# Branch C's norm reciprocals all in the first two blocks of branch A, one product piece behind the masked products, and two evacuations in halves

## Chip, core and metric

The kernel runs on one core of one Trainium2 chip. The metric is device time in microseconds (us) of one execution.

## What is computed

One layer of a decoder trunk with four token mixers in parallel, and a final norm; 1024 tokens, model width 1024, branch width 256, all in float32:

```
hn = rmsnorm(x) * (1 + scale) + shift              # scale, shift, gate from c @ w_mod
u  = hn @ w_in                                     # 59 column tiles of 128
ya = rwkv7(...)     * silu(ag)     # branch A: 4 heads of 64, a recurrence over time
yb = hgrn2(...)     * silu(bg)     # branch B
yc = retention(...) * silu(cg)     # branch C: 4 heads, chunks of 128
yd = rglru(...)     * silu(dg)     # branch D
# inside retention, at its end, with 4 heads of 64 columns:
o  = o * rsqrt(mean(o * o over the head) + 1e-6) * ret_norm_g
merged = sum_b sigmoid(mg_b) * (y_b @ w_branch[b]) # 32 merge tiles: 4 branches x 8 column tiles
out = rmsnorm(x + gate * (merged @ w_out)) * final_g
```

## The kernel before

The program is written by hand, one instruction stream per engine, ordered by semaphores. An engine works strictly in the order of its text; a wait holds everything behind it.

**TensorE (PE).** The tiles of `u` are made one after the other in the order of the list `BULK`, two 512-column halves each, with every float32 product taken as three (hn_hi by w_hi, hn_lo by w_hi, hn_hi by w_lo, L590). `project_part(0..3)` makes a quarter of a tile. From `fill` on, a *merge tile* is cut into ten pieces: pieces 0 to 7 are six products each of the gate tile, 8 and 9 are six products each of y @ w_branch (L639). `fill(n)` issues the next n pieces; it is the work that PE does while other engines work on a branch. Piece 0 waits for the evacuation of the tile before it (`s_evac`) and for the weights (`s_w_lo_ready`).

**Branch A** runs in four block pairs, s = 0..3, each over 256 tokens: `rwkv_products` transposes slots (L860, in `turn`), ScalarE (ACT) copies the results to SBUF (L1377, L1380), PE makes the masked products (L884), VectorE (DVE) masks and combines them (L1917 to L1933). `rwkv_inverse` then has five levels: PE products (L910), DVE L1940 or L1943, PE products (L915), DVE L1950 and L1952. After that come four rounds, `rwkv_chunk`, k = 0..3: PE L970 and L978, DVE's two additions L1975 (`s_a_sa_ready`), PE L988 to L997, DVE L1982, L1986, L1989. In round 1 DVE also runs `prep_queries(s + 1)` (L1879 to L1889), in round 2 `prep_keys(s + 1)` (L1897), which sets `s_a_ends_ready`; PE waits for that ahead of the next pair's transposes. A block pair takes 40 pieces, four merge tiles; pair 0 begins in tile 0 at piece 4, so tile 4 starts in round 3 of pair 0.

**Branch C** ends just before pair 0: its eight steps (i = 0..7) go through PE L830 to L848 with a `project_part(i % 4)` in each, ACT copies each result (L1331), and after steps 3 and 7 ACT evacuates the whole tile (`evac(1)`, two instructions at L1235, of which the second tile is Silu). Then ACT squares (L1340), computes the exponentials that branch A needs (`decays(0)`, L1361 to L1366) and takes the roots (L1348). The reciprocals of the roots are eight pieces on DVE, `ret_norm(z)` (L1904), z = 0..3 in slot 16 and 4..7 in slot 17. They are spread over the work of DVE in pair 0.

**GpSimd (POOL)** splits each weight tile into w_hi (a cast, L505) and w_lo (L507), two halves per tile; the first half waits until PE has used up the first half of the tile before (`s_w_first_used`), the second until that tile is done (`s_proj_done`). Behind the weights it splits the branch weights (L515, L517), and at merge tile 0 branch D's y (L476, two instructions). After merge tiles 2 and 3 it finishes branch C in its own order: wait for `s_ret_norm_ready` at 4 and at 8, then L533, L535, L539, L541, L476, a *series* of five operations over 128x1024.

**SyncE** issues the loads of the weights, each behind the split that frees its buffer. ACT and DVE also take the merge tiles' sigmoid (L1257) and products (L1858, or L1861 and L1863).

Of the kernel before, what the change touches and what calls it, by code (L numbers as in the profile page):

```python
# [99 lines left out]
def build(nc, ins, out_d):  # L100
    x_d, w_mod_d, w_in_d, w_branch_d, w_out_d = (ins[n] for n in ("x", "w_mod", "w_in", "w_branch", "w_out"))
    with ExitStack() as ctx:
# [443 lines left out]
        def _(pe):  # L546
# [63 lines left out]
            def fill(count):  # L610

                for _ in range(count):
                    merge_piece(state["piece"] % 10)
                    state["piece"] += 1
# [245 lines left out]
            def rwkv_products(s):  # L862
                if s:
                    pe.wait_ge(s_a_y_ready, 4 * s)
                    pe.wait_ge(s_a_g_ready, 4 * s)
                pe.wait_ge(s_a_ends_ready, s + 1)
                for b in range(2):
                    ts = slice((2 * s + b) * P, (2 * s + b + 1) * P)
                    for q, src in enumerate((12, 13, 4, 5)):
                        last = turn(bank[4 + 2 * b][:, q * P:(q + 1) * P], slot(src)[:, ts])  # L870
                    last.then_inc(s_a_tm1_done, 1)
                    for q, src in enumerate((14, 15, 10, 11)):
                        last = turn(bank[5 + 2 * b][:, q * P:(q + 1) * P], slot(src)[:, ts])
                    last.then_inc(s_a_tm2_done, 1)
                fill(3)
                pe.wait_ge(s_a_tm_ready, 4 * s + 4)
                for b in range(2):
                    for a, src in enumerate((14, 10)):
                        for j in range(2):
                            for c in range(2):  # L880
                                t64 = slice((2 * s + b) * P + c * C, (2 * s + b) * P + (c + 1) * C)
                                for par in range(2):
                                    r = slice(64 * par, 64 * par + 64)
                                    last = mm(bank[4 + 2 * b + par][64 * c:64 * c + 64,  # L884
                                                                    (2 * a + j) * P:(2 * a + j + 1) * P],
                                              slot(src + j)[r, t64], slots[r, j:j + 5:4, t64], start=True, stop=True)
                    last.then_inc(s_a_m_done, 1)
                fill(4)

            def each(f):  # L890
                for b in range(2):
# [255 lines left out]
        def _(act):  # L1147
# [74 lines left out]

            def evac(count):
                for _ in range(count):
                    bi = state["bi"]
                    ct = BULK[bi]
                    banks = (0, 1) if bi % 2 == 0 else (2, 3)
                    for n in range(2):
                        act.wait_ge(s_proj_done, 2 * bi + n + 1)
                        src = bank[banks[n]][:, :]  # L1230
                        if ct in (BF, BF + 1):
                            nc.scalar.activation(b_f_raw[ct - BF][:, halves(n)], src, ACT.Copy).then_inc(s_evac, 1)
                            act.wait_ge(s_evac, after(s_evac))
                        else:
                            nc.scalar.activation(slot(PROJ[ct])[:, halves(n)], src,  # L1235
                                                 ACT.Silu if ct in GATED else ACT.Copy).then_inc(s_evac, 1)
                            after(s_evac)
                    state["bi"] += 1

            def evac_turned(ct, turned):  # L1240
                bi = BULK_AT[ct]
# [85 lines left out]
                after(s_kz_tm_ready)  # L1327
            evac_turned(CV + 1, 1)
            for i in range(NT):
                act.wait_ge(s_ret_o_done, i + 1)  # L1330
                nc.scalar.activation(pair(18)[:, :, i * P:(i + 1) * P],  # L1331
                                     bank[7][:, 0:256].rearrange("p (j t) -> p j t", j=2), ACT.Copy)\
                    .then_inc(s_ret_o_ready, 1)
                act.wait_ge(s_ret_o_ready, after(s_ret_o_ready))
                if i % 4 == 3:
                    evac(1)

            def squares(src, tmp):
                for j in range(2):
# [34 lines left out]
            for s in range(NT // 2):  # L1374
# [29 lines left out]
                for k in range(4):  # L1404
                    n = 4 * s + k
# [147 lines left out]
        def _(dve):  # L1553
# [346 lines left out]
            def ret_norm(z):  # L1900

                dve.wait_ge(s_roots, 4 + z // 2 + 1)
                q = slot(16 + z // 4)[:, 256 * (z % 4):256 * (z % 4 + 1)]
                nc.vector.reciprocal(q, q).then_inc(s_ret_norm_ready, 1)  # L1904
                dve.wait_ge(s_ret_norm_ready, after(s_ret_norm_ready))
# [7 lines left out]
            for s in range(NT // 2):  # L1913
# [22 lines left out]
                for l in range(1, 6):  # L1936
                    dve.wait_ge(s_a_v_done, 5 * s + l)
                    v_new = bank[5][:, 0:256].rearrange("p (n t) -> p n t", t=32)
                    if l < 5:
                        nc.vector.tensor_tensor(v_lev, v_new, table(tb("lev")[:, 32 * l - 32:32 * l], 8), MUL)\  # L1940
                            .then_inc(s_a_v_ready, 1)
                    else:
                        nc.vector.tensor_copy(v_lev, v_new).then_inc(s_a_v_ready, 1)  # L1943
                    dve.wait_ge(s_a_v_ready, after(s_a_v_ready))
                    if l in (1, 4):
                        merge_half(1)
                    dve.wait_ge(s_a_dx_done, 5 * s + l)
                    du = bank[6][:, 0:256].rearrange("p (n t) -> p n t", t=32)
                    if l < 5:
                        nc.vector.tensor_tensor(Ud, Ud, du, ADD).then_inc(s_vector_step, 1)  # L1950
                        dve.wait_ge(s_vector_step, after(s_vector_step))
                        nc.vector.transpose(Td, Ud).then_inc(s_a_x_ready, 1)  # L1952
                        dve.wait_ge(s_a_x_ready, after(s_a_x_ready))
                        if l == 3:
                            merge_half(0)
                    else:
                        dve.wait_ge(s_a_uu_ready, 2 * s + 2)
                        for c in range(2):
                            r = slice(64 * c, 64 * c + 32)
                            done = s_vector_step if c == 0 else s_a_x_ready  # L1960
                            nc.vector.tensor_copy(UU[r, :, 32:64], du[r]).then_inc(done, 1)
                            dve.wait_ge(done, after(done))
                    if s == 0:
                        ret_norm(l - 1)
                for k in range(4):
                    b, c = k // 2, k % 2
                    i, n = 2 * s + b, 4 * s + k
                    rc = slice(64 * c, 64 * c + 64)
                    if s == 0 and k < 3:
                        ret_norm(5 + k)  # L1970
                    dve.wait_ge(s_a_wg_done, n + 1)
                    dve.wait_ge(s_a_u_ready, s + 1)
                    for par in range(2):
                        u = pair(14)[rc, :, i * P + C * par:i * P + C * (par + 1)]
                        nc.vector.tensor_tensor(u, u, bank[6 + par][rc, 0:128].rearrange("p (j v) -> p j v", j=2),  # L1975
                                                ADD).then_inc(s_a_sa_ready, 1)
                    if k == 3:
                        merge()
                    dve.wait_ge(s_a_y_done, 2 * n + 2)
                    dve.wait_ge(s_a_y_part, n + 1)  # L1980
                    y = pair(4)[:, :, n * C:(n + 1) * C]
                    nc.vector.tensor_tensor(y, y, bank[6][:, 256:384].rearrange("p (j t) -> p j t", j=2), ADD)\  # L1982
                        .then_inc(s_a_y_ready, 1)
                    dve.wait_ge(s_a_y_ready, after(s_a_y_ready))
                    dve.wait_ge(s_a_gnew_done, n + 1)
                    nc.vector.tensor_tensor(G, G, bank[5][:, 0:P], ADD).then_inc(s_vector_step, 1)  # L1986
                    dve.wait_ge(s_vector_step, after(s_vector_step))
                    g2 = G.rearrange("p (j v) -> p j v", j=2)
                    nc.vector.tensor_tensor(g2, g2, e_end[:, s % 2, k, :].unsqueeze(2).to_broadcast([P, 2, C]), MUL)\  # L1989
                        .then_inc(s_a_g_ready, 1)  # L1990
                    dve.wait_ge(s_a_g_ready, after(s_a_g_ready))
                    if k == 0:
                        merge()
                    elif k == 1 and s + 1 < NT // 2:
                        prep_queries(s + 1)
                    elif k == 2 and s + 1 < NT // 2:
                        prep_keys(s + 1)
# [268 lines left out]
```

## Time and profile before

| | us |
|---|---|
| median of 3 runs | 1095.77 (1094.17 to 1098.38) |
| the profiled execution | 1097.14 |
| its span, first to last instruction | 1095.0 |
| PE busy | 1058.5 |
| DVE, ACT, POOL busy | 592.4, 304.9, 373.6 |

The span is what the views of the trace show; 2.1 us of the profiled execution lie outside it. Times within views count from the start of the span. PE is TensorE's matmuls, DVE VectorE, ACT ScalarE, POOL GpSimd. A bracket at the end of a row of a timeline is the time for which the engine stood idle before that row, and what released it. L-numbers are lines of the kernel before.

### The profile page before, as it was taken

How to read it: one execution, taken by the hardware profiler on the slowest of the kernel's cores; microseconds unless marked ns; L12 is line 12 of the kernel's file. 1: busy time of each engine (PE TensorE's matmuls, PEld its weight loads, DVE VectorE, ACT ScalarE, POOL GpSimd, SP SyncE). 2: the span in 40 equal slices, each digit the busy share in tenths (PEclk: the TensorE clock that was granted, in tenths of full speed). 3: DMA queues.
4: the chain of work that ended last, by engine and by line, in shares of the span. 5: the costliest groups of instructions: out<-in, count | busy, mean ns of one | idle time of the engine just before them, and what ended most of it. 6: DMA issues, size and time to landing. Idle time of an engine off the chain costs nothing.

```text
span 1095.0 us, 22343 instructions
## 1 busy us (share of the span) xinstructions
PE 1058.5 (97%) x9736; PEld 830.6 (76%) x9736; DVE 592.4 (54%) x976; ACT 304.9 (28%) x497; POOL 373.6 (34%) x343
## 2 busy tenths in 40 slices
PE   7999999999999799999999999999999999999997
PEld 5686787767677677877877777877778777888885
DVE  3768933976455152353442118557777586423543
ACT  5545113321502102202201034244545341001221
POOL 1431543321435421222222232344334239762000
PEclk9999999999999899999999999999999999999999
DMA  9700111210110110110111121120101026412221
GB/s 355 263 21 10 48 49 49 77 29 25 40 28 25 34 41 26 35 41 25 35 41 31 30 68 39 39 59 26 51 26 50 26 86 246 129 36 96 96 77 58
DMA packets 80129, 70.25 MB, mean 64 GB/s; under 512 B 4128, under 2 KB 68896, under 8 KB 80032
## 3 DMA queue, kind: packets, MB, share of 16 engines
q1 hardware_dynamic: 74560, 49.35, 14.6%
q10 hardware_dynamic: 5472, 19.47, 4.8%
q8 instruction: 77, 1.26, 0.5%
q14 instruction: 20, 0.16, 0.0%
HBM read 64.61 MB, written 4.19 MB: 63 GB/s over the span
## 4 chain that ended last, share of the span: by engine, by line
PE 84%; DVE 9%; POOL 3%; DMA 1%; ACT 1%; issue 1%; SPq 1%; ACTq 0%; DVEq 0%; POOLq 0%
PE bank L590 52%; PE bank L1123 8%; PE bank L639 6%; PE bank L691 2%; PE bank L1078 1%; DVE slots L1706 1%; DMA slots<-in_w_mod 1%; PE bank L910 1%; PE bank L915 1%; DVE tab L1924 1%; PE bank L796 1%; DVE stage L1917 1%; PE bank L860 1%; POOL y_lo L476 1%; DVE slots L1690 1%
## 5 line engine op out<-in xcount | busy, mean ns | idle before, releaser
L590 PE MATMUL bank<-hn_hi,w_hi 128*128 128x512 f32 x880 | 360.9, 410 | 10.4 <-POOL w_lo L507 7.6
L590 PE MATMUL bank<-hn_hi,w_lo 128*128 128x512 f32 x880 | 344.6, 392 | 0.0
L590 PE MATMUL bank<-hn_lo,w_hi 128*128 128x512 f32 x880 | 344.6, 392 | 0.0
L505 POOL CAST w_hi<-w_raw 128x512 fp32r<-128x512 f32 x110 | 86.1, 783 | 537.1 <-PE bank L590 537.1
L590 PEld LDWEIGHTS bank<-hn_hi,w_hi 128*128 128x128 f32 x880 | 165.8, 188 | 51.8 <-issue 12.5
L590 PEld LDWEIGHTS bank<-hn_hi,w_lo 128*128 128x128 f32 x880 | 165.9, 189 | 36.4
L590 PEld LDWEIGHTS bank<-hn_lo,w_hi 128*128 128x128 f32 x880 | 166.2, 189 | 33.2 <-issue 1.9
L507 POOL TENSOR_TENSOR w_lo<-w_raw,w_hi 128x512 fp32r<-128x512 f32 x110 | 155.4, 1413 | 8.8
L1257 ACT ACTIVATE stage<-bank 128x512 f32<-128x512 f32 x64 | 38.2, 600 | 208.0 <-PE bank L590 189.4
L1861 DVE TENSOR_TENSOR stage<-stage,bank 128x512 f32<-128x512 f32 x48 | 33.0, 687 | 50.2 <-PE bank L639 48.9
L1235 ACT ACTIVATE slots<-bank 128x512 f32<-128x512 f32 x42 | 24.6, 599 | 123.0 <-PE bank L590 122.9
L639 PE MATMUL bank<-y_hi,w_branch_hi 128*128 128x512 f32 x128 | 51.3, 401 | 0.0
L1123 PE MATMUL bank<-out_w_hi,hn_hi 128*128 128x512 f32 x128 | 49.9, 390 | 0.2 <-DVE hn_lo L2156 0.2
L639 PE MATMUL bank<-y_lo,w_branch_hi 128*128 128x512 f32 x128 | 50.0, 391 | 0.0
L639 PE MATMUL bank<-y_hi,w_branch_lo 128*128 128x512 f32 x128 | 50.0, 390 | 0.0
L1123 PE MATMUL bank<-out_w_lo,hn_hi 128*128 128x512 f32 x128 | 49.8, 389 | 0.0
L1123 PE MATMUL bank<-out_w_hi,hn_lo 128*128 128x512 f32 x128 | 49.8, 389 | 0.0
L1863 DVE TENSOR_TENSOR slots<-slots,stage 128x512 f32<-128x512 f32 x48 | 42.1, 878 | 1.7
L1917 DVE TENSOR_TENSOR stage<-bank,tab 128x512 f32<-128x512 f32 x16 | 9.9, 684 | 41.3 <-PE bank L884 41.3
L2172 DVE TENSOR_TENSOR fin_tmp<-bank,slots 128x512 f32<-128x512 f32 x16 | 11.1, 692 | 38.2 <-PE bank L1123 38.1
L517 POOL TENSOR_TENSOR w_branch_lo<-w_branch,w_branch_hi 128x256 fp32r<-128x256 f32 x32 | 28.0, 875 | 2.6
L691 PE MATMUL bank<-hn_hi,w_hi 128*128 128x512 f32 x64 | 26.4, 413 | 2.4 <-DVE hn_lo L1616 2.4
(320 smaller groups left out, 1546.5 us busy)
## 6 DMA issues: line engine op xcount, KB each, us to landing
w_raw<-in_w_in SPq DMA_DIRECT2D x110, 256.0 KB, 2.8
slots<-in_w_mod SPq DMA_DIRECT2D x16, 512.0 KB, 11.4
slots<-in_x SPq DMA_DIRECT2D x8, 512.0 KB, 9.5
w_branch<-in_w_branch SPq DMA_DIRECT2D x32, 128.0 KB, 2.8
slots<-in_w_mod ACTq DMA_DIRECT2D x8, 512.0 KB, 5.2
slots<-in_w_out ACTq DMA_DIRECT2D x8, 512.0 KB, 6.3
xr<-in_x ACTq DMA_DIRECT2D x8, 512.0 KB, 3.5
out<-xr ACTq DMA_DIRECT2D x8, 512.0 KB, 2.6
```

The source lines that it names most:

```text
L505: nc.gpsimd.tensor_copy(w_hi[p][:, :, :], w_raw[p][:, :, :]).then_inc(s_pool_step, 1)
L507: nc.gpsimd.tensor_tensor(w_lo[p][:, :, :], w_raw[p][:, :, :], w_hi[p][:, :, :].bitcast(F32), ALU.subtract).then_inc(s_w_lo_ready, 1)
L517: nc.gpsimd.tensor_tensor(w_branch_lo[h][:, :, :], w_branch[h][:, :, :], w_branch_hi[h][:, :, :].bitcast(F32), ALU.subtract)\
L590: last = mm(o, w[p][:, k4, :], h[:, k, n * HALF:(n + 1) * HALF], start=(p == 0 and k4 == 0 and q == 0), stop=(p == 1 and k4 == 3 and q == 2))
L639: last = mm(o, w[:, k, :], h[:, k, :], start=(k == 0 and q == 0), stop=(k == 1 and q == 2))
L691: last = mm(bank[q][:, :], w[p][:, k4, cols], h[:, k, n * HALF:(n + 1) * HALF], start=(k == 0 and z == 0), stop=(k == KT - 1 and z == 2))
L1123: last = mm(bank[(2 * tt + n) % 8][:, :], m[tt % 2][:, k * P:(k + 1) * P], w[k][:, n * HALF:(n + 1) * HALF], start=(k == 2 and q == 0), st ...
L1235: nc.scalar.activation(slot(PROJ[ct])[:, halves(n)], src, ACT.Silu if ct in GATED else ACT.Copy).then_inc(s_evac, 1)
L1257: nc.scalar.activation(sig[n], bank[(6 if mi == AHEAD else 0) + n][:, :], ACT.Sigmoid).then_inc(s_evac, 1)
L1861: nc.vector.tensor_tensor(sig[n], sig[n], bank[(4 if mi == AHEAD else 2) + n][:, :], MUL).then_inc(s_vector_step, 1)
L1863: nc.vector.tensor_tensor(o, o, sig[n], ADD).then_inc(s_merged, 1)
L1917: nc.vector.tensor_tensor(kinds(b)[:, par].rearrange("p a j t -> p (a j) t"), bank[4 + 2 * b + par][:, :].rearrange("p (h t) -> p h t", h= ...
```

## The change

The eight reciprocals of branch C are put elsewhere in DVE's order of pair 0: numbers 1 and 3 stand inside levels 2 and 3 of the inverse, between the two products of a level; 0, 2, 4, 5 and 6 follow levels 1 to 5; 7 stands ahead of round 0. Before, 0 to 4 followed the levels, and 5, 6 and 7 stood ahead of rounds 0, 1 and 2. In `rwkv_products`, in all four block pairs, PE issues two pieces ahead of the masked products and five behind, instead of three and four. ACT evacuates the two tiles that are projected during the retention steps in halves: the first half after the copy of step 2 (and 6), the second half ahead of the wait for step 3's (and 7's) result; before, both halves came after the copy of step 3 (and 7).

```diff
@@ rwkv_products (PE)
                     last.then_inc(s_a_tm2_done, 1)
-                fill(3)
+                fill(2)
                 pe.wait_ge(s_a_tm_ready, 4 * s + 4)
...
                     last.then_inc(s_a_m_done, 1)
-                fill(4)
+                fill(5)
@@ ACT
             def evac(count):
                 for _ in range(count):
-                    bi = state["bi"]
+                    evac_halves((0, 1))
+
+            def evac_halves(ns):
+                for bi in (state["bi"],):
                     ct = BULK[bi]
                     banks = (0, 1) if bi % 2 == 0 else (2, 3)
-                    for n in range(2):
+                    for n in ns:
                         act.wait_ge(s_proj_done, 2 * bi + n + 1)
...
-                    state["bi"] += 1
+                    state["bi"] += ns[-1]
...
             for i in range(NT):
+                if i % 4 == 3:
+                    evac_halves((1,))
                 act.wait_ge(s_ret_o_done, i + 1)
...
-                if i % 4 == 3:
-                    evac(1)
+                if i % 4 == 2:
+                    evac_halves((0,))
@@ DVE, branch A, levels l = 1..5
                     if l in (1, 4):
                         merge_half(1)
+                    elif s == 0 and l < 4:
+                        ret_norm(2 * l - 3)
                     dve.wait_ge(s_a_dx_done, 5 * s + l)
...
                     if s == 0:
-                        ret_norm(l - 1)
+                        ret_norm((0, 2, 4, 5, 6)[l - 1])
                 for k in range(4):
...
-                    if s == 0 and k < 3:
-                        ret_norm(5 + k)
+                    if s == 0 and k == 0:
+                        ret_norm(7)
                     dve.wait_ge(s_a_wg_done, n + 1)
```

## Rows read from the trace of the kernel before

**Rows 1.** The page, part 1: busy time, share and instructions, TensorE first.
```profile
PE 1058.5 (97%) x9736; PEld 830.6 (76%) x9736; DVE 592.4 (54%) x976; ACT 304.9 (28%) x497; POOL 373.6 (34%) x343
```
**Rows 2.** PE's waits: for whom, us in total, times, longest us.
```profile
PE bank L590 <- POOL w_lo L507: 7.6, 2, 5.9
...
PE bank L910 <- DVE wa L1933: 2.6, 4, 0.6
```
**Rows 3.** Windows: length, PE, PEld, DVE, ACT, POOL busy, granted clock, DMA share, GB/s.
```profile
260.00:280.00 20.00, 18.34 (x100) 13.58 (x96) 8.83 (x13) 5.69 (x9) 7.30 (x7) 1.00 0.12 33
...
360.00:380.00 20.00, 14.94 (x82) 12.13 (x83) 0.89 (x4) 2.07 (x4) 9.55 (x10) 0.74 0.14 39
```
**Rows 4.** PE's timeline, pair 0, round 3: start, us, operation, idle before.
```profile
357.54 0.50 PE L639 MATMUL bank<-y_hi,w_branch_hi 128*128 128x512 f32 x1
...
365.06 0.76 PE L590 MATMUL bank<-hn_hi,w_hi 128*128 128x512 f32 x1 [5.86 <-POOL w_lo L507]
...
375.99 1.91 PE L860 MATMUL bank<-tab,slots 128*128 128x128 f32 x16
```
**Rows 5.** PE's timeline, pair 1, round 3.
```profile
447.54 0.50 PE L639 MATMUL bank<-y_hi,w_branch_hi 128*128 128x512 f32 x1
...
455.85 1.91 PE L860 MATMUL bank<-tab,slots 128*128 128x128 f32 x16
```
**Rows 6.** POOL's timeline, the second series and the split of merge tile 4.
```profile
351.70 2.37 POOL L533 TENSOR_TENSOR slots<-slots 128x1024 f32<-128x1024 f32 x1 [11.38 <-DVE slots L1904]
...
357.10 2.39 POOL L539 TENSOR_TENSOR slots<-slots 128x1024 f32<-128x1024 f32 x1
...
360.68 2.34 POOL L476 TENSOR_TENSOR y_lo<-slots,y_hi 128x1024 fp32r<-128x1024 f32 x1
...
363.65 1.26 POOL L507 TENSOR_TENSOR w_lo<-w_raw,w_hi 128x512 fp32r<-128x512 f32 x1
```
**Rows 7.** DVE's timeline, pair 0: level 2's addition, two reciprocals, the eighth.
```profile
309.32 0.42 DVE L1950 TENSOR_TENSOR tab<-tab,bank 128x256 f32<-128x256 f32 x1 [1.85 <-PE bank L915]
...
327.91 3.54 DVE L1904 RECIPROCAL slots<-slots 128x256 f32<-128x256 f32 x2
...
349.88 1.75 DVE L1904 RECIPROCAL slots<-slots 128x256 f32<-128x256 f32 x1
```
**Rows 8.** POOL's timeline, pair 1, rounds 0 and 1.
```profile
428.79 0.74 POOL L517 TENSOR_TENSOR w_branch_lo<-w_branch,w_branch_hi 128x256 fp32r<-128x256 f32 x1
...
438.99 1.60 POOL L507 TENSOR_TENSOR w_lo<-w_raw,w_hi 128x512 fp32r<-128x512 f32 x1
```
**Rows 9.** DVE's timeline, pair 0, round 1.
```profile
346.82 0.29 DVE L1989 TENSOR_TENSOR stage<-stage,tab 128x128 f32<-128x128 f32 x1
...
349.08 0.88 DVE L1889 SCALAR_TENSOR_TENSOR slots<-slots,par 128x256 f32<-128x256 f32 x2
```
**Rows 10.** DVE's timeline, pair 1, round 1.
```profile
439.49 1.78 DVE L1889 SCALAR_TENSOR_TENSOR slots<-slots,par 128x256 f32<-128x256 f32 x2
```
**Rows 11.** DVE's timeline ahead of pair 0.
```profile
281.62 1.29 DVE L1879 TENSOR_TENSOR slots<-slots 128x504 f32<-128x504 f32 x1 [4.71 <-ACT slots L1366]
...
285.07 0.69 DVE L1897 TENSOR_TENSOR slots<-slots,tab 128x512 f32<-128x512 f32 x1
```
**Rows 12.** POOL's timeline at the same time: branch D's y.
```profile
277.68 4.70 POOL L476 TENSOR_TENSOR y_lo<-slots,y_hi 128x1024 fp32r<-128x1024 f32 x2
```
**Rows 13.** PE's timeline, pair 0, round 2.
```profile
352.84 0.34 PE L988 MATMUL bank<-stage,slots 64*64 64x64 f32 x4
```
**Rows 14.** The chain that ended last: start, us, what; three pieces of pair 1.
```profile
377.90 4.13 PE bank L590 x18
```
**Rows 15.** PE's timeline, pair 1, level 1.
```profile
390.28 0.75 PE L910 MATMUL bank<-wa,stage 32*32 32x32 f32 x64 [0.64 <-DVE wa L1933]
```
**Rows 16.** PE's timeline, the first fill, and the transposes of pair 0.
```profile
276.97 0.50 PE L590 MATMUL bank<-hn_hi,w_hi 128*128 128x512 f32 x1 [1.66 <-ACT slots L1235]
...
286.03 1.91 PE L860 MATMUL bank<-tab,slots 128*128 128x128 f32 x16
```

## What I expect of the change, and why

> **What bounds the kernel now.** Part 1 of the page comes first: TensorE (PE) is busy for 1058.5 of the 1095.0 us of the span [rows 1], so a change pays only where PE stands still or runs slowly. The table of PE's waits names the places. The longest single one is 5.9 us, for the split of a weight tile on POOL (w_lo, L507); four waits of 0.6 us, 2.6 in all, are for DVE's transpose at L1933 [rows 2]. The table of windows shows the granted clock next: 0.74 between 360 and 380 us, against 1.00 elsewhere, as between 260 and 280 [rows 3]. So the long wait costs twice, once as idle time and once as work at 1.2 GHz instead of 2.4.
>
> I price it by comparing two block pairs of branch A, not from the wait alone. The last round of pair 0 runs from its first merge product at 357.54 to the transposes of the next pair at 375.99, 18.45 us [rows 4]. The same instructions in pair 1, which has no reciprocals of branch C, run from 447.54 to 455.85, 8.31 us [rows 5]. The difference is **10.14 us**; 5.86 of it is the idle time in [rows 4], the other 4.28 the low clock.
>
> Why is the weight split late? POOL's timeline shows it idle for 11.38 us until 351.70, released by DVE's L1904, and then busy with a series of five operations that is over at 360.68 + 2.34 = 363.0. Only then comes the split of merge tile 4, ready at 363.65 + 1.26 = 364.9 [rows 6]. PE starts at 365.06. The eighth reciprocal, `ret_norm(7)`, ends at 349.88 + 1.75 = 351.63 [rows 7]: it is what POOL waits for.
>
> **Part 1: the reciprocals.** Their number (eight) and size stay. In the new order 0 and 2 follow levels 1 and 2, 1 and 3 stand inside levels 2 and 3, 4 and 5 follow levels 3 and 4, 6 follows level 5, and 7 stands ahead of the first round. DVE has 1.85 us of idle before the level's last addition [rows 7]; a reciprocal of 1.75 goes into it, so numbers 1 and 3 cost nothing. If they overran by a tenth, PE still has two pieces of fill before it wants the result. Behind level 5 there are two reciprocals now, 327.91 to 331.45 [rows 7]; they become numbers 6 and 7. So the eighth ends at 331.5 on the clock of before, 20 us earlier, and the ones ahead of rounds 1 and 2 vanish from DVE.
>
> POOL's queue decides how much of this is usable. The first series (after tile 2) needs reciprocals 0 to 3 and can start some 6 us sooner, into time in which POOL was idle. The second stands behind the split of tile 3, whose second half waits for PE to use up tile 2. Pair 1 gives that time undisturbed: the split of the branch weights ends at 428.79 + 0.74 = 429.53 [rows 8], and the last rounds of the pairs are 90.00 us apart [rows 4, 5], so 339.5 here. The series takes 363.0 - 351.7 = 11.3 us [rows 6] and is over at 350.9; the first half of tile 4 is ready near 353. PE wants it after the six products that start at 357.54, so at about 359. **The 5.9 us stall goes, with 6 us to spare, and with it the low clock: -10.1 us.** What is late next is below.
>
> **The collision this makes.** In its new place the second series runs beside `prep_queries(1)` in round 1. Today POOL is idle there. What does DVE pay? The pair L1889, with two operands in SBUF, takes 0.88 us at 349.08, when POOL is idle, but 1.78 at 439.49, when POOL's w_lo runs from 438.99; and that w_lo takes 1.60 instead of the 1.26 at 363.65 [rows 6, 8 to 10]. L1879, issued at 281.62, ends at 282.91, just behind POOL's y_lo, which ends at 282.38 [rows 11, 12]. So they take turns, a whole instruction at a time: DVE ends at the end of POOL's plus its own length less 0.17, and POOL starts about 0.14 before DVE's end.
>
> Worked through: the series starts at 339.6. By the offsets of [rows 6], L539 runs until 347.4 and L541 until 348.5. DVE reaches L1989 at 346.82 [rows 9], is held by L539 and free at 347.5; L1879 ends at 349.0; POOL's y_lo (2.34) at 351.2; L1882 at 351.75; the cast of w_hi (the 0.6 between 363.02 and 363.65) at 352.2; L1884 at 352.7; w_lo (1.26) at 353.9; the pair L1889 at 354.6; the two additions L1975 at 355.1 (0.5, an estimate: each touches half the partitions of an operation like L1989, 0.29). PE wants these additions at 352.84, where it starts L988 [rows 13]. **New wait: +2.3 us.** Bounds: 0, if DVE wins the early turns, because the undisturbed list ends before 352; 3.3, if POOL's operations all start as late as they can. I take 2.3, since the rows closest in kind (439.49, 281.62) show waits of whole instructions. The delayed split of tile 4 still ends at 353.9, 5 us ahead of need. The first series meets only operations with one SBUF operand (reciprocals, transposes, additions from PSUM), and costs nothing.
>
> The Trainium skill (SBUF — State Buffer, section "Who interferes with whom") says of this that VectorE with two SBUF inputs and a GpSimd operation that reads SBUF hold a shared port one after the other, each for its whole instruction, and that issue order decides. It speaks against the new place of the series: by it the 2.3 stands, without it this term is 0 and the sum 1082.9. The rows just told bear it out for POOL's two-input operations and casts.
>
> **Part 2: the moved piece.** PE runs two pieces ahead of the masked products (L884) and five behind, instead of three and four. A group of three lasts 4.13 us [rows 14], one piece 1.38. DVE's chain L1917 to L1933 starts 1.38 us sooner, PE's fills end when they did, and PE's idle time of 0.64 ahead of L910 [rows 15] falls away, four times: **-2.6 us**. Ahead of L884 PE also waits for four copies by ACT (L1377, L1380); they take about 2 us behind the transposes, and two pieces are 2.75, so nothing is exposed. The pieces keep their order, so the gates, the merges and POOL's splits stay where PE's work puts them. The price could run from 0 (DVE delayed elsewhere) to -2.9.
>
> **Part 3: the halves.** At round 3 of the retention it hides work that was hidden. At round 7 the two halves (1.1 us) leave the end: PE's wait of 1.66 us ahead of the first fill [rows 16] goes, and ACT is about 1.0 us earlier with the squares, exponentials and roots. But the next point at which PE waits is `s_a_ends_ready` ahead of the transposes at 286.03 [rows 16]. That comes from DVE's L1897, 285.07 + 0.69 = 285.76, which goes back to L1879 [rows 11]. L1879 would be issued near 280.7, and POOL's y_lo of branch D holds it until 282.38 as before [rows 12]. So the transposes can only come at about 285.8: **-0.2 us**, and the rest turns into waiting there. If DVE isn't held, it is up to -1.4. The table load that Silu needs moves into an idle stretch of ACT.
>
> **Sum**, against the profiled execution (1097.14 us, span 1095.0): -10.1 + 2.3 - 2.6 - 0.2 = -10.6, so 1086.5 for an execution like it. It lies 1.4 above the median of the runs, 1095.77; the same difference from there gives **1085.2 us**. Everything behind the changed places waits for PE and moves as a block.
>
> **Rivals.**
> - *No collision* (0.22): DVE wins its turns or has cover for them. For it: L1989 and the addition before it are short, and the order of issue is tight. Against: [rows 9 to 12]. The sum is -12.9: 1082.9; with all of part 3 as well, 1081.7.
> - *The new wait also lowers the clock* (0.10): PE stands still for 2.3 us or more at L988, and the 5.86 us stall was followed by 1.2 GHz, which cost 4.28. For it: the products around the wait are small. Against: the wait of 1.66 us stands in a window with a clock of 1.00 [rows 3, 16]. 1085.2 + 4.3 = 1089.5.
> - *It doesn't do what it says* (0.09): the series is still late, because something ahead of it in POOL's queue (a DMA of tile 3, a turn with DVE) holds it 7 us or more. Then part 2 and a part of the stall count: 1091 to 1094. Against: the rows show POOL with nothing to do from 340.3 on but to wait for L1904.
> - *Slower* (0.03): the wait at L988 brings the low clock, and PE, which then has short waits at every level of the next inverse, doesn't get it back. The low level lost 4.28 us within the 10.9 between 365.06 and 375.99, 0.4 per us. To be 5.5 us slower than before it has to eat 10.6 + 5.5 = 16.1 us, so it decides from 40 us with such a clock, pair 1's whole inverse: 1101.3. Against: today the clock is back before 375.99, during the same kind of work.
>
> **How the numbers follow.** The forecast has 0.56. Its own bounds (collision 0 to 3.3, parts 2 and 3) give 1082 to 1088. The range reaches over the first rival and to the second's figure: 1081.5 to 1089.5, which leaves out the third, the fourth and the tails. 0.5% is 5.5 us, about what a measurement of this kernel can tell from no change. Below 1090.3 lie the forecast and two rivals, 0.87; within 0.5%, the third and a remainder, 0.10; slower 0.03.
>
> **What would show it.** The wait of L590 for POOL near 359 is gone, and no window between 340 and 400 has a clock below 1.00. POOL's second series begins right behind the split of tile 3's branch weights. L1904 is eight times 1.75, and the last ends within 4 us of L1961. PE has a new wait for DVE's L1975 ahead of L988 in round 2 of pair 0, and L1879, L1882, L1884 and L1889 there last 1 to 3 us each instead of 0.4 to 0.7. The four waits for L1933 are gone. The wait for ACT's L1235 ahead of the first fill is gone, but a wait of about 1 us for DVE's L1897 stands ahead of L860. I am wrong if the stall of L590 remains (queue), if L988 doesn't wait (turns), or if the clock falls anywhere new.

## The result, and the profile after

The changed kernel takes 1087.61 us (median of 4 runs, 1087.14 to 1089.75), the kernel before 1095.66 beside it: a ratio of 0.9924, 95% interval 0.9909 to 0.9939. Forecast were 1085.2 us and a range of 1081.5 to 1089.5. The profiled execution took 1087.85 us, its span is 1086.0, 9.0 less than before.

All lines of DVE behind the two inserted ones have moved by 5 to 7: L1904, L1924, L1975, L1879 to L1889 and L1897 of before are L1909, L1929, L1982, L1884 to L1894 and L1902 now. First PE's waits (us in total, times, longest), as in [rows 2]:

```profile
PE bank L988 <- DVE slots L1982: 2.1, 1, 2.1
PE bank L590 <- POOL w_lo L507: 1.8, 1, 1.8
PE bank L860 <- DVE slots L1902: 1.5, 1, 1.5
```

The 5.9 us for POOL are gone (the 1.8 are another place, near 900 us), the four waits for L1933 are gone, and two waits are new. The windows show the clock around the new wait at L988 (length, busy PE, PEld, DVE, ACT, POOL, granted clock, DMA share, GB/s), against [rows 3]:

```profile
320.00:340.00 20.00, 20.00 (x329) 15.65 (x328) 9.83 (x15) 6.68 (x13) 14.09 (x12) 1.00 0.06 18
340.00:360.00 20.00, 17.87 (x150) 13.84 (x149) 11.85 (x18) 3.03 (x5) 14.21 (x9) 0.91 0.11 31
360.00:380.00 20.00, 20.00 (x191) 16.27 (x190) 7.14 (x17) 3.54 (x7) 4.82 (x6) 1.00 0.12 34
```

PE's timeline in round 2 and at the start of round 3 of pair 0, which answers to [rows 13]:

```profile
355.10 0.34 PE L988 MATMUL bank<-stage,slots 64*64 64x64 f32 x4 [2.13 <-DVE slots L1982]
...
356.22 0.78 PE L590 MATMUL bank<-hn_hi,w_hi 128*128 128x512 f32 x1
356.80 0.63 PE L590 MATMUL bank<-hn_lo,w_hi 128*128 128x512 f32 x1
...
359.36 0.55 PE L639 MATMUL bank<-y_lo,w_branch_hi 128*128 128x512 f32 x1
...
361.38 0.50 PE L639 MATMUL bank<-y_hi,w_branch_hi 128*128 128x512 f32 x1
```

From 356.2 to 359.6 the products take 0.63 us each, at 1.2 GHz, then 0.39 again, at 2.4 GHz. Why PE waits can be read from DVE and POOL side by side; first DVE in round 1, as in [rows 9]:

```profile
346.88 0.66 DVE L1996 TENSOR_TENSOR stage<-stage,tab 128x128 f32<-128x128 f32 x1
347.58 1.46 DVE L1884 TENSOR_TENSOR slots<-slots 128x504 f32<-128x504 f32 x1
348.96 2.87 DVE L1887 TENSOR_TENSOR slots<-slots,tab 128x512 f32<-128x512 f32 x1
351.75 1.09 DVE L1889 TENSOR_TENSOR slots<-slots 128x512 f32<-128x512 f32 x1
352.88 1.76 DVE L1894 SCALAR_TENSOR_TENSOR slots<-slots,par 128x256 f32<-128x256 f32 x2
354.57 0.47 DVE L1982 TENSOR_TENSOR slots<-slots,bank 64x128 f32<-64x128 f32 x2
```

and POOL's second series, as in [rows 6]:

```profile
339.54 2.45 POOL L533 TENSOR_TENSOR slots<-slots 128x1024 f32<-128x1024 f32 x1
...
345.02 2.38 POOL L539 TENSOR_TENSOR slots<-slots 128x1024 f32<-128x1024 f32 x1
347.46 1.04 POOL L541 CAST y_hi<-slots 128x1024 fp32r<-128x1024 f32 x1
348.58 2.70 POOL L476 TENSOR_TENSOR y_lo<-slots,y_hi 128x1024 fp32r<-128x1024 f32 x1
351.22 1.08 POOL L505 CAST w_hi<-w_raw 128x512 fp32r<-128x512 f32 x1
352.39 1.59 POOL L507 TENSOR_TENSOR w_lo<-w_raw,w_hi 128x512 fp32r<-128x512 f32 x1
```

The series now begins at 339.54 right behind the branch weights of tile 3, and w_lo of tile 4 is ready at 353.98, 9 us before PE wants it. Each DVE instruction ends about half a microsecond after one of POOL's: 349.04 after 348.50, 351.83 after 351.28, 352.84 after 352.30. Undisturbed, L1884 to L1894 took 2.8 us; here it is 7.1. The length of DVE's list alone doesn't make the wait: in the kernel before, the same list with a reciprocal more in it was through with the additions at 352.13, ahead of PE's 352.84 in [rows 13]:

```profile
351.65 0.48 DVE L1975 TENSOR_TENSOR slots<-slots,bank 64x128 f32<-64x128 f32 x2
```

By stages the 9.00 us are these, before against after:

| from, to | before | after | difference | forecast |
|---|---|---|---|---|
| start to the split of tile 0's second half | 274.42 | 275.08 | +0.66 | 0 |
| to the transposes of pair 0 (L860) | 11.61 | 11.81 | +0.20 | -0.2 |
| L860 to L910, the four pairs together | 57.14 | 54.31 | -2.83 | -2.6 |
| pair 0: L910 to the next L860 | 75.71 | 69.20 | -6.51 | -7.8 |
| the rest | | | -0.52 | 0 |

The first line isn't the change's doing: the copy of retention step 2, ahead of ACT's first changed instruction, is already 0.70 us late (250.15 instead of 249.45), and a second profile of the changed kernel (changed_again, below) has 274.37. What lies behind pair 0 scatters too: from the L860 after it to the end of the span that second profile takes 719.31 us, where this one takes 716.32. The three lines between compare equal work. Pair 1 may stand for the third: L860 at 369.68, L910 at 383.23, 13.55 us, where [rows 4] and [rows 15] give 14.29.

### The profile page after: what moved, and what is told of

It reads as the page before. It is cut to its first block, busy times and chain, and to the rows that moved or that the text cites. A ratio compares the mean times of both kernels' runs of the same rounds, so it can differ in the third digit from the quotient of the medians.

```text
span 1086.0 us, 22343 instructions
## 1 busy us (share of the span) xinstructions
PE 1054.8 (97%) x9736; PEld 828.2 (76%) x9736; DVE 592.2 (55%) x976; ACT 305.1 (28%) x497; POOL 374.8 (35%) x343
## 3 DMA queue, kind: packets, MB, share of 16 engines
q8 instruction: 77, 1.26, 0.5%
## 4 chain that ended last, share of the span: by engine, by line
PE 86%; DVE 7%; POOL 2%; ACT 1%; DMA 1%; issue 1%; SPq 1%; ACTq 0%; DVEq 0%; POOLq 0%
PE bank L590 53%; PE bank L1123 8%; PE bank L639 7%; PE bank L691 2%; PE bank L1078 1%; DVE slots L1711 1%; DMA slots<-in_w_mod 1%; PE bank L910 1%; PE bank L915 1%; PE bank L860 1%; DVE slots L1695 1%; PE bank L884 1%; PE bank L796 1%; POOL y_lo L476 1%; PE bank L988 1%
## 5 line engine op out<-in xcount | busy, mean ns | idle before, releaser
L1982 DVE TENSOR_TENSOR slots<-slots,bank 64x128 f32<-64x128 f32 x32 | 7.8, 282 | 40.1 <-ACT slots L1405 24.9
```

## The experiments

Each kernel was timed four to six times, beside the kernel before on the same chip. Single executions of one kernel spread by 2 us and more, so for differences of 1 to 3 us I go by the trace, and the medians only bear it out.

**p1_order_only**: the kernel before with the new order of the reciprocals alone.

```diff
+                    elif s == 0 and l < 4:
+                        ret_norm(2 * l - 3)
...
-                        ret_norm(l - 1)
+                        ret_norm((0, 2, 4, 5, 6)[l - 1])
...
-                    if s == 0 and k < 3:
-                        ret_norm(5 + k)
+                    if s == 0 and k == 0:
+                        ret_norm(7)
```

> The kernel before with the reciprocals' new order alone; the moved piece and the halves are undone. Theory (parts add up; the stall of tile 4 goes, 10.1 us, and a wait of 2.1 us at L988 in round 2 of pair 0 comes, with 1.6 us of low clock behind it): 6.4 us below the kernel before, some 1089.2, the wait of 2.1 us at L988 there as in the changed kernel, four waits of 0.6 for L1933 back. Rival (the wait at L988 comes from the moved piece or from the earlier evacuation, which shift DVE against POOL): no wait at L988, some 1085.6.

1090.59 us against 1096.92, ratio 0.9943 (0.9931 to 0.9956): 6.3 us less. The wait at L988 is there, 2.1 us. The rival falls: the wait belongs to part 1. The profiled execution is the longest of the five (1092.82): its clock stayed low for longer behind the wait, and from L988 to the next L860 it took 16.12 us (354.87 to 370.99), where the same instructions took 12.99 at full clock (changed_again, 354.40 to 367.39). That is 3.1 us of low clock, not the 1.6 expected.

**p2_piece_only**: `fill(2)` and `fill(5)` alone.

```diff
-                fill(3)
+                fill(2)
...
-                fill(4)
+                fill(5)
```

> The kernel before with one piece moved behind the masked products, nothing else. Theory: 0.7 us less between the transposes and the first products of level 1 in each of four block pairs, the stall of 5.9 us unchanged: 2.8 us less, some 1092.9. Rival (the gain goes elsewhere: the stall of tile 4 grows by what PE comes sooner, since POOL's series does not move): pair 0's 0.7 us are lost again in a longer stall, 2.1 us less, some 1093.6.

1091.86 us against 1096.92, ratio 0.9960 (0.9947 to 0.9972): 5.1 us less, more than the theory's 2.8 or the rival's 2.1. PE's table of waits says that the stall neither grew nor shrank:

```profile
PE bank L590 <- POOL w_lo L507: 7.6, 2, 5.9
```

POOL's series hangs on DVE, and DVE on PE, so it came sooner by as much. The other 2.7 us of the profiled span are in the low clock behind the stall: from round 3's first merge product to the next transposes it is 356.52 to 372.25, 15.73 us instead of the 18.45 of [rows 4]. Whether the shorter low stretch comes with this arrangement (all five runs are short) or by chance stays open.

**p12_no_halves**: the changed kernel without part 3.

```diff
-                if i % 4 == 3:
-                    evac_halves((1,))
...
-                if i % 4 == 2:
-                    evac_halves((0,))
+                if i % 4 == 3:
+                    evac(1)
```

> The changed kernel with both evacuations of the retention back behind steps 3 and 7. Theory (DVE's L1884 is held by POOL's y_lo of branch D whenever it is issued, so the halves give nothing): within 0.3 us of the changed kernel; a wait of 1.7 us for ACT ahead of the first fill, and none for DVE's L1902 ahead of the transposes of pair 0. Rival (the halves give what they take out of PE's wait): 1.4 us more than the changed kernel, some 1089.0.

1088.81 us against 1096.92, ratio 0.9922 (0.9907 to 0.9937), the changed kernel's own 0.9924. From the split of tile 0's second half to L860 it takes 11.61 us, 0.20 less than with the halves. The median lies 1.2 us above the changed kernel's 1087.61 and by itself would speak for the rival, but the kernel before is 1.3 us higher in these rounds too, and the five runs without the halves spread over 3.8 us; I go by the stretch. So the halves gave nothing here. In this profile the wait at L988 is again 2.1 us, but the clock stays:

```profile
340.00:360.00 20.00, 17.85 (x169) 13.72 (x168) 12.18 (x20) 3.32 (x6) 15.38 (x11) 1.00 0.07 21
```

**last3_early**: reciprocals 5, 6 and 7 together ahead of round 0, the others as before.

```diff
-                    if s == 0 and k < 3:
-                        ret_norm(5 + k)
+                    if s == 0 and k == 0:
+                        for z in (5, 6, 7):
+                            ret_norm(z)
```

> The kernel before with reciprocals 5, 6 and 7 together ahead of round 0 of pair 0, the first five where they were. Theory (only the eighth counts, and the second series starts behind tile 3's split anyway): the stall of tile 4 goes; the second series starts 0.8 us later than in the changed kernel, so the wait at L988 is 2.9 instead of 2.1 us; with the low clock 5.6 us below the kernel before, some 1090.1. Rival (the first series must be early too, or DVE's three in a row delay the additions of round 0): tile 4 still waits 2 us or more, or a wait of up to 1.8 us for DVE stands in round 0: 1092 to 1094.

1091.75 us against 1096.92, ratio 0.9957 (0.9944 to 0.9971): 5.2 us less. The wait at L988 is 2.9 us, as forecast, round 0 has none, and the stall of tile 4 is gone. So the place of the last three, of which POOL waits for the eighth, is what counted. The rest of the new order only brings the second series some 0.7 us forward (counted from L860, it starts after 54.16 us here and 53.47 in p1_order_only).

**prep_early**: `prep_queries(1)` behind round 1's additions, beside POOL's L535.

```diff
                                                 ADD).then_inc(s_a_sa_ready, 1)
+                    if s == 0 and k == 1:
+                        prep_queries(1)
...
-                    elif k == 1 and s + 1 < NT // 2:
+                    elif k == 1 and 0 < s < NT // 2 - 1:
                         prep_queries(s + 1)
```

> The changed kernel with prep_queries(1) directly behind the two additions of round 1 of pair 0 (beside POOL's L535, one operand in SBUF) instead of at the round's end (beside L539, L541, L476). Theory (DVE with two SBUF operands takes turns with POOL's two-input operations and casts, not with L535): L1884 to L1894 take some 2.8 us together instead of 6.7, no wait at L988, no window below 1.00: 3.7 us less than the changed kernel, some 1083.9. Rival 1 (every POOL operation holds DVE, L535 too): L1884 is held until L535's end, the y additions come late, and PE waits 2 us or more at L970 of round 2: 1087 or more. Rival 2 (the wait at L988 is not POOL's doing but the length of DVE's list): no change, 1087.6.

1088.76 us against 1096.59, ratio 0.9933 (0.9920 to 0.9946): no gain over the changed kernel, and from L910 to the next L860 pair 0 takes 67.57 us, where changed_again takes 67.61. The wait moved to L970 (1.9 us). DVE in round 1:

```profile
341.94 0.96 DVE L1884 TENSOR_TENSOR slots<-slots 128x504 f32<-128x504 f32 x1
342.82 0.68 DVE L1887 TENSOR_TENSOR slots<-slots,tab 128x512 f32<-128x512 f32 x1
343.42 0.68 DVE L1889 TENSOR_TENSOR slots<-slots 128x512 f32<-128x512 f32 x1
344.14 3.88 DVE L1894 SCALAR_TENSOR_TENSOR slots<-slots,par 128x256 f32<-128x256 f32 x2
...
348.69 1.69 DVE L1998 TENSOR_TENSOR stage<-stage,tab 128x128 f32<-128x128 f32 x1
```

and POOL beside it:

```profile
341.25 2.85 POOL L535 TENSOR_SCALAR slots<-slots,par 128x1024 f32<-128x1024 f32 x1
344.18 2.38 POOL L539 TENSOR_TENSOR slots<-slots 128x1024 f32<-128x1024 f32 x1
```

L1887 and L1889 ran undisturbed beside L535, so my theory of which operations hold DVE was right but for L1884 (0.96 us instead of 0.68), and rival 1 is wrong in that; its consequence, the wait at L970, came all the same, by another way. The pair L1894 was issued 0.04 us before L539 and even so lost 3 us to it and to the cast; then L1998, the scaling of branch A's state, met the next L476. I had counted time beside L535 for the whole list, and it was just too short.

**piece_in_wait**: one piece of round 2 ahead of L988.

```diff
-                fill(1 if n == 15 else 2)
+                fill(1 if n == 15 else 3 if n == 2 else 2)
...
-                    fill(3 if n % 4 == 3 else 2)
+                    fill(3 if n % 4 == 3 else 1 if n == 2 else 2)
```

> The changed kernel with one piece of round 2 of pair 0 issued ahead of L988 instead of behind L997, so that PE's idle time there is 0.75 instead of 2.13 us, the work being the same. Theory (the idle time of 2.1 us is what brings the low clock): clock 1.00 throughout, 1.4 + 1.6 = 3.0 us less, some 1084.6. Rival (the clock falls at this place whatever the wait, from the small products around it): 1.4 us less, some 1086.2, and a window of 340 to 360 still below 1.00.

1085.92 us against 1096.59, ratio 0.9910 (0.9896 to 0.9924). The wait is 0.8 us, as worked out, and the clock of its window 1.00. From L910 to the next L860 pair 0 takes 66.42 us, 1.2 less than in changed_again, which kept its clock there too. Since the clock can also stay with the full wait (p12_no_halves), this one profile doesn't separate the theories; the median is 1.7 us below the changed kernel's, between the 3.0 and the 1.4 expected.

**ylo_early**: POOL's y_lo of branch D between the halves of tile 0's split.

```diff
                 for p in range(2):
+                    if p == 1 and BULK[bi] == MG + 8 * 3 + 4:
+                        for j in range(2):
+                            split_y(3, j, slice(0, T), 1 + j)
...
-                    if merge in (0, 16):
+                    if merge == 16:
...
```

> The changed kernel with POOL's y_lo of branch D (L476, two instructions, 4.7 us) between the two halves of tile 0's split, where POOL stands idle, instead of behind tile 0's branch weights. Theory (it holds L1884 in front of pair 0): L1884 takes 0.7 instead of 2.4 us, the wait of 1.5 us for L1902 ahead of L860 goes, 1.5 us less, some 1086.1. Rival (the wait there comes from ACT's exponentials): the wait stays within 0.3 us of 1.5, 1087.6.

1086.68 us against 1096.59, ratio 0.9916 (0.9902 to 0.9929). L1884 (L1887 here) is free, and nothing waits ahead of the transposes (L863 here):

```profile
280.24 0.68 DVE L1887 TENSOR_TENSOR slots<-slots 128x504 f32<-128x504 f32 x1 [3.66 <-ACT slots L1374]
...
284.19 1.91 PE L863 MATMUL bank<-tab,slots 128*128 128x128 f32 x16
```

From tile 0's split (274.07) it is 10.12 us, 1.69 less than in the changed kernel.

**ylo_no_halves**: ylo_early without part 3.

> ylo_early with both retention evacuations back behind steps 3 and 7. Theory (the halves bring 1.5 us once nothing holds L1884): the first fill waits 1.7 us for ACT, nothing waits ahead of L860, and from the second half of tile 0's split to L860 it takes 11.6 us instead of ylo_early's 10.1: 1.5 us more than ylo_early. Rival (the halves never bring anything): as ylo_early within 0.3 us in that stretch.

1087.71 us against 1097.37, ratio 0.9920 (0.9902 to 0.9938). The stretch takes 11.59 us, 1.47 more than in ylo_early. So the halves are worth 1.5 us once POOL's y_lo is out of DVE's way, and cost 0.2 before.

**both_early**: prep_early and ylo_early together.

> prep_early and ylo_early together. Theory (independent turns at two places): 3.7 + 1.5 = 5.2 us less than the changed kernel, some 1082.4, and no wait of PE over 1.3 us between 200 and 600 us. Rival (the places are coupled through POOL's queue): less than 4 us.

1086.15 us against 1096.59, ratio 0.9912 (0.9898 to 0.9927). It carries on prep_early's wait (2.0 us at L970), this time with the clock at 0.91, and ylo_early's gain (10.14 us from tile 0's split to the transposes). The 5.2 us forecast were missed because prep_early's 3.7 didn't come.

**changed_again**: the changed kernel once more.

> The changed kernel once more, beside the next three. The wait of 2.1 us at L988 is there again in every theory. Theory (what follows the wait is by chance: the clock may fall or stay, as it did in two kernels with the same wait): its runs spread over some 2 us, around 1088, and those with a lower mean clock are the longer ones. Rival (the spread has another source): clock and time of the runs are not related.

1087.79 us against 1097.37, ratio 0.9914 (0.9899 to 0.9929). The same wait, but another clock behind it:

```profile
354.40 0.34 PE L988 MATMUL bank<-stage,slots 64*64 64x64 f32 x4 [2.13 <-DVE slots L1982]
...
359.08 0.50 PE L639 MATMUL bank<-y_hi,w_branch_hi 128*128 128x512 f32 x1
```

From L988 to round 3's first merge product it is 4.68 us here and 6.28 (355.10 to 361.38) in the profile above, of the same program. That prices the low clock of that execution at 1.60 us. The five runs of changed_again took 1088.5, 1088.1, 1087.8, 1086.9 and 1086.9 us at mean clocks of 0.996, 0.997, 0.997, 0.998 and 0.998; those of p12_no_halves go from 1086.0 at 0.999 to 1089.9 at 0.995 and 0.996 (with one of 1088.8 at 0.994). So a lower clock goes with a longer time, but not only through L988: the profiled execution here is the longest of its five (1088.5), and its clock fell near 746 us instead, in a later part of the program that the change doesn't touch:

```profile
745.62 0.53 PE L1078 MATMUL bank<-slots 64*32 64x32 f32 x38 [1.42 <-issue]
...
745.00:750.00 5.00, 4.38 (x48) 3.51 (x48) 3.59 (x10) 2.08 (x10) 0.00 (x0) 0.66 0.01 3
```

The same happened in both_early and prep_split (behind 1.53 us of idle time, near 803 and 801 us) and in prep_early (behind 1.85 us, near 906). Such falls move from execution to execution, and a difference of 1 to 2 us between two whole spans can't be put down to an edit.

**prep_split**: as prep_early, but the pair L1894 in round 2.

```diff
+                if s != 1:
+                    prep_bonus(s)
+
+            def prep_bonus(s):
...
+                    if s == 0 and k == 1:
+                        prep_queries(1)
...
-                    elif k == 1 and s + 1 < NT // 2:
+                    elif k == 1 and 0 < s < NT // 2 - 1:
                         prep_queries(s + 1)
                     elif k == 2 and s + 1 < NT // 2:
+                        if s == 0:
+                            prep_bonus(1)
                         prep_keys(s + 1)
```

`prep_bonus` is the pair L1894; `prep_queries(1)` no longer contains it.

> The changed kernel with the first three operations of prep_queries(1) (L1884 to L1889 of the changed kernel) right behind round 1's additions, and its last pair (L1894) in round 2 in front of prep_keys(1). Theory (the three fit beside POOL's L535, which did not hold them in prep_early; the pair is what ran into L539): L1884 to L1889 take 2.2 us, no wait of PE at L988 or L970 over 0.5 us, clock 1.00 between 340 and 360: 2.1 us less than the changed kernel where that one kept its clock, 3.7 where not; a median some 2.9 lower, 1084.9. Rival (some DVE operation always meets one of POOL's in this round): a wait of 1.5 us or more at L970 or L988.

1086.07 us against 1097.37, ratio 0.9901 (0.9884 to 0.9917): 1.7 us below changed_again, where 2.9 were forecast. In the changed place the forecast holds: from L910 to the next L860 it takes 65.44 us, 2.17 less than in changed_again (2.1 forecast) and 3.76 less than in the first profile (3.7). PE waits neither at L988 nor at L970, and is busy throughout the window:

```profile
340.00:360.00 20.00, 20.00 (x189) 15.37 (x189) 8.93 (x21) 3.31 (x6) 14.99 (x11) 1.00 0.13 37
```

**split_and_ylo**: prep_split and ylo_early together.

> prep_split and ylo_early together. Theory: the two places add up, 1.5 us less than prep_split, some 1083.4, with neither the wait for L1902 ahead of L860 nor those at L988 and L970. Rival (coupled): as prep_split within 0.5 us.

**1083.66 us** (1083.15 to 1083.98) against 1097.37, ratio 0.9877 (0.9858 to 0.9896): 4.1 us below the changed kernel in the same rounds, the best of all. By the trace the two places add up: 10.14 us from tile 0's split to the transposes, as in ylo_early and both_early, and 65.61 us from L910 to the next L860, as in prep_split but for 0.2. The median is 2.4 us below prep_split's, more than the 1.5 forecast; prep_split's profiled execution had the fall of the clock near 801 us, this one has no window below 1.00 before 1070 us.

## Why the prediction was right, and where it was off

**The stall and its price: right.** The 10.14 us went as a whole, and tile 4 is now 9 us early (I said 6, leaving out that the new wait and the low clock behind it also delay PE). p1_order_only gives it alone, with the wait: its profile has 75.71 - 70.89 = 4.82 us less from L910 to the next L860, and -10.1 + 2.1 + 3.1, its own low clock, is -4.9. That its median of -6.3 meets my -6.4, which has 1.6 for the clock, is in part luck, since the clock's share changes from execution to execution.

**The collision: right, and it is what kept the span's gain from being 9.0 + 2.1 + 1.6 = 12.7 us.** I worked out that the additions would end at 355.1 and PE wait 2.3 us; L988 starts at 355.10 after 2.13. The turns came in the order given. prep_split shows the cause: the same POOL series and the same DVE instructions, with L1884 to L1889 some 5 us sooner (341.79 instead of 347.58) and the pair in the next round (353.86, 0.88 us long), and no wait.

**The clock: the term that was missing.** The forecast left it at full speed and gave the low clock 0.10; a fall anywhere new was among its own signs of being wrong, and it came. This step failed, though the time stayed in the range. The first profile shows the clock low for some 3 us behind the wait, for 1.6 us, not 4.28. It isn't fixed: with the same wait of 2.1 us it fell in four of six profiles (after, p1_order_only, ylo_early, ylo_no_halves; not in p12_no_halves and changed_again), and it cost 1.6 us in three of them and 3.1 in p1_order_only. It fell behind last3_early's 2.9 us, and behind the 2.0 us at L970 in both_early but not in prep_early. My argument from the 1.66 us wait in [rows 3, 16] was no argument, since one execution with a full clock doesn't exclude the fall; elsewhere it fell behind 1.42 us. It should have been a term of 0 to 4.3 us in the sum. What decides whether the clock falls stays open. (The last rival's 0.4 per us is low as well: the products run fast again from 373.9, so the 4.28 us were lost in 8.8 us, 0.5 per us. Its time doesn't rest on it.)

**Part 2: right, -2.83 for -2.6.** The idle of 0.64 went four times, plus some 0.07 each of the step from a fill to L910. p2_piece_only gives it alone in the trace, 13.57 us instead of 14.25 in pair 0.

**Part 3: the mechanism was right, the sign not.** L1884 is held by y_lo of branch D as forecast (281.25, issued early, 2.36 us). But a second turn came, which I didn't have:

```profile
285.77 0.98 DVE L1902 TENSOR_TENSOR slots<-slots,tab 128x512 f32<-128x512 f32 x1
```

with POOL's cast beside it:

```profile
285.52 0.68 POOL L505 CAST w_hi<-w_raw 128x512 fp32r<-128x512 f32 x1 [2.44 <-PE bank L590]
```

Since PE used up tile 0's first half sooner, POOL's cast for tile 1 came 0.8 us sooner (285.52 instead of 286.32; 1.5 counted from tile 0's split) and held the last instruction that PE waits for. So -0.2 became +0.2. The step that failed is the one that let POOL's work stand still while PE's moved.

**Sum.** The span moved by 9.0 us instead of 10.6. Of what has a cause, 1.6 of clock and 0.4 of part 3 stand against 0.2 of part 2 and 0.3 in pair 0 (0.2 of it the wait of 2.13 for 2.3): 1.5 less than forecast. The 0.7 at the start and the 0.5 in the rest nearly cancel, and two profiles of the same program differ by as much and more in these places. The medians moved by 8.1.

## What to carry to other kernels

When a stall is removed by doing work sooner, lay the moved work beside every other engine's at its new time, not only beside the one that waited for it: here a series on POOL went from a stretch in which DVE had little to do into a dense one. Two engines that take turns can be priced from their timelines, here to 0.2 us (2.13 for 2.3), as long as each instruction meets the one it was laid beside; prep_early missed by its whole 3.7 us because one pair came just too late. The cure was to put the short list beside an instruction that hardly holds it, and the pair into another round. Count a new wait of PE twice, once for itself and once, with a chance, for the clock behind it. And compare single executions by stretches of equal work, since the clock can fall in any of several places.

## What the runs showed of the hardware

- The granted clock can fall behind a wait of 2.1 us of PE, and need not: in two executions of the same program the following stretch took 4.68 and 6.28 us. It also fell behind 1.42 us (changed_again), 1.53 (both_early, prep_split), 1.85 (prep_early) and 2.90 (last3_early), and in the kernel before it stayed at 1.00 behind 1.51 us at 756.61 and 1.72 at 916.02. Behind the same stall of 5.86 us the stretch took 18.45 us in the kernel before and 15.73 in p2_piece_only.
- POOL's L535 (one tensor with a scalar per partition, 2.85 us) holds DVE's two-operand instructions only for about its first 1.1 us. In prep_early L1884, issued at 341.94 beside L535 at 341.25, ends at 342.90, which by the rule of turns is a release at 342.4; those after it run in their 0.68. both_early, prep_split and split_and_ylo give the same 1.1, and so does the kernel before, where an instruction of 0.29 us beside L535 at 354.17 took 0.96:

```profile
354.47 0.96 DVE L1989 TENSOR_TENSOR stage<-stage,tab 128x128 f32<-128x128 f32 x1
```

POOL's two-tensor operations and casts held DVE to their end (348.50, 351.28, 352.30 above). The prediction's "each for its whole instruction" is too wide for L535; there the measurement decides.
- POOL pays as well: beside DVE its w_lo took 1.59 us instead of 1.26, and its cast 1.08 instead of 0.61.
